# Where the two parts of the norm's operand lie in a partition, and the experts' stationary tiles

## The reference

```python
def rmsnorm(x, g):
    x32 = x.astype(jnp.float32)
    y = x32 * lax.rsqrt(jnp.mean(x32 * x32, axis=-1, keepdims=True) + EPS)
    return (y * g.astype(jnp.float32)).astype(x.dtype)

def swiglu(x, wg, wu, wd):
    return (jax.nn.silu(x @ wg) * (x @ wu)) @ wd

def moe(x, router, wg, wu, wd):
    ...
    for e in range(N_EXPERTS):
        y = y + gates[..., e:e + 1].astype(x.dtype) * swiglu(x, wg[e], wu[e], wd[e])
    return y
```

## The kernel before

| streamed operand | before | after |
|---|---|---|
| `uh`, k = 0 to 6 | 352 | 352 |
| `uh`, k = 7 | 384 | 384 |
| `ul`, k = 0 to 6 | 480 | 352 |
| `ul`, k = 7 | 0 | 0 |
| `hid`, `gop`, `mp`, `ret`, `mixp`, `plep`, `pleU`: both parts | 96 | 352 |
| `whi`, `wlo` as the streamed operand | 288 | 288 |

## Time and profile before

### The profile page before, as it was taken

One profiled execution on the slowest core, in us unless ns is written; L12 is line 12 of the kernel. 1 busy time (PEld: TensorE's weight loads), 2 busy tenths in 40 slices (PEclk: granted clock), 3 DMA queues, 4 the chain that ended last, 5 costly groups with the idle time before them and its releaser, 6 DMA issues.

```text
span 2169.2 us, 37238 instructions
## 1 busy us (share of the span) xinstructions
PE 2112.1 (97%) x15426; PEld 1971.2 (91%) x15426; DVE 1529.8 (71%) x2191; ACT 1366.4 (63%) x1887; POOL 65.4 (3%) x102
## 2 busy tenths in 40 slices
PE   8999999999999999999999999999989999999999
PEld 7988999999989899998888888888879999978999
DVE  5777556765567675565999999976867665875664
ACT  6765475544567654755877777776756545775553
POOL 0003000000000130000000000000000000000000
PEclk9999999999999999998999999999999999999999
DMA  7434345566554343453989999954315565423553
GB/s 262 152 99 138 100 148 177 183 183 193 166 169 149 101 141 97 151 181 149 343 323 329 333 330 333 350 190 156 122 49 180 183 199 164 156 69 127 195 185 136
DMA packets 126450, 400.69 MB, mean 185 GB/s; under 512 B 26048, under 2 KB 26432, under 8 KB 126272
## 3 DMA queue, kind: packets, MB, share of 16 engines
q1 hardware_dynamic: 126272, 398.20, 55.1%
HBM read 395.79 MB, written 2.36 MB: 184 GB/s over the span
## 4 chain that ended last, share of the span: by engine, by line
PE 86%; ACT 6%; DVE 5%; issue 1%; POOL 1%; DMA 0%; SPq 0%; ACTq 0%; DVEq 0%; POOLq 0%
PE ps L492 85%; DVE wlo L2164 2%; ACT scr L1411 2%; ACT whi L1401 1%; ACT arena L1411 1%; DVE arena L2172 1%; DVE arena L2164 1%; DVE scr L2164 1%; ACT L1411 1%; ACT L1405 0%; PE ps L1084 0%; ACT rst L1411 0%; DVE h L2164 0%; ACT uh L1411 0%; POOL arena L3134 0%
## 5 line engine op out<-in xcount | busy, mean ns | idle before, releaser
L2164 DVE TENSOR_TENSOR wlo<-raw,whi 128x1024 fp32r<-128x1024 f32 (+2 forms) x622 | 746.1, 1213 | 288.8 <-ACT whi L1401 283.5
L1401 ACT ACTIVATE whi<-raw 128x1024 fp32r<-128x1024 f32 (+2 forms) x622 | 642.9, 1042 | 315.1 <-PE ps L492 310.0
L492 PE MATMUL ps<-uh,whi 128*128 128x256 f32 x2240 | 647.5, 289 | 12.6 <-DVE arena L2172 4.2
L492 PE MATMUL ps<-uh,wlo 128*128 128x256 f32 x2240 | 633.1, 283 | 0.0
L492 PE MATMUL ps<-ul,whi 128*128 128x256 f32 x2240 | 626.8, 280 | 0.0
L492 PE MATMUL ps<-arena_r,whi 128*128 128x256 f32 x2720 | 477.5, 280 | 2.9 <-DVE arena_r L2164 2.0
L492 PEld LDWEIGHTS ps<-uh,whi 128*128 128x128 f32 x2240 | 421.3, 188 | 25.7 <-issue 14.7
L492 PEld LDWEIGHTS ps<-ul,whi 128*128 128x128 f32 x2240 | 422.9, 189 | 5.6 <-issue 5.3
L492 PEld LDWEIGHTS ps<-arena_r,whi 128*128 128x128 f32 x2720 | 415.0, 189 | 6.8 <-DVE arena_r L2164 3.4
L492 PEld LDWEIGHTS ps<-uh,wlo 128*128 128x128 f32 x2240 | 420.5, 188 | 0.0
L492 PE MATMUL ps<-arena_r,wlo 128*128 128x256 f32 x1360 | 378.3, 278 | 0.0
(11 more groups left out here) (183 smaller groups left out, 2229.4 us busy)
## 6 DMA issues: line engine op xcount, KB each, us to landing
raw<-stream SPq DMA_DIRECT2D x586, 512.0 KB, 4.2
arena<-stream SPq DMA_DIRECT2D x64, 512.0 KB, 5.8
CO<-stream SPq DMA_DIRECT2D x44, 512.0 KB, 5.4
raw<-stream SPq DMA_DIRECT2D x32, 384.0 KB, 4.3
arena<-stream SPq DMA_DIRECT2D x20, 384.0 KB, 4.2
CO<-stream SPq DMA_DIRECT2D x12, 384.0 KB, 4.6
CO<-const SPq DMA_DIRECT2D x2, 704.5 KB, 6.1
h<-xT SPq DMA_DIRECT2D x4, 256.0 KB, 5.8
```

Of the source, the lines that this page charges most:

```text
L492: return self.e.matmul(o, l, r, start=start, stop=stop, skip_group_check=True)
L1401: self.e.activation(M.whi[:, b:b + n], M.raw[a][:, 0:n], ACT.Copy).then_inc(K.sem("weight_hi"), 1)
L2164: return self.e.tensor_tensor(o, a, b, op)
```

## The change

`Tiles` gets its step as an argument: `uh` keeps 8 numbers for tile 7, `ul` gets 8 + 32 = 40 (160 bytes). Both tensors grow from 2080 to 2176 numbers (8704 bytes, 17 x 512), so that `ul` starts at byte 108832 and its tiles 0 to 6 lie like those of `uh` modulo 512. The router's two parts move from tensors of their own into the last 64 numbers of `uh` and `ul`. All that is made later moves up by 256 bytes: the scratch tensors, and the arena from byte 136288 to 136544. In the arena, `UG[0]` becomes two dense tensors of 2048 numbers that begin at 288 modulo 512 (before: 160 and 288, with a last tile 32 bytes further), and `HT` behind them starts 32 numbers further in the arena. No instruction is added, taken away or moved, and no wait.

```diff
--- before.py
+++ after.py
@@ -22,6 +22,8 @@
 AHEAD = 3
 OFF = 16
 STEP = 8
+TURN = 32
+LINE = 128
 ARENA = 23128
 CAP = 128
 ALL = slice(None)
@@ -180,22 +182,19 @@
 
 
 
-    def __init__(self, ap, c0=0, c1=T):
-        self.ap, self.c0, self.c1 = ap, c0, c1
+    def __init__(self, ap, step):
+        self.ap, self.step = ap, step
 
     def __getitem__(self, ix):
 
         p, k, c = ix
-        c0, c1 = self.c0 + (c.start or 0), self.c1 if c.stop is None else self.c0 + c.stop
+        c0, c1 = c.start or 0, T if c.stop is None else c.stop
         if isinstance(k, slice):
             assert k.stop == k.start + 2 and k.start % 2 == 0
-            n = T + (STEP if k.stop == 8 else 0)
+            n = T + (self.step if k.stop == 8 else 0)
             return v3(self.ap[p, k.start * T:k.start * T + 2 * n], n)[:, :, c0:c1]
-        at = k * T + (STEP if k == 7 else 0)
+        at = k * T + (self.step if k == 7 else 0)
         return self.ap[p, at + c0:at + c1]
-
-    def columns(self, c0, c1):
-        return Tiles(self.ap, c0, c1)
 
 
 class Steps:
@@ -297,10 +296,10 @@
         self.SM, self.CO = sb("SM", small_layout()[1]), sb("CO", const_layout()[1])
         raw = sb("raw", NRAW * CH)
         self.whi, self.wlo = sb("whi", NSPLIT * CH, F32R), sb("wlo", NSPLIT * CH, F32R)
-        self.h, uh, ul = sb("h", 2048), sb("uh", 2048 + 2 * OFF, F32R), sb("ul", 2048 + 2 * OFF, F32R)
-        self.hT, self.U = v3(self.h), tuple(Tiles(x[:, OFF:2048 + 2 * OFF]) for x in (uh, ul))
+        self.h, uh, ul = sb("h", 2048), sb("uh", 2048 + LINE, F32R), sb("ul", 2048 + LINE, F32R)
+        self.hT, self.U = v3(self.h), tuple(Tiles(x[:, OFF:2048 + LINE], n) for x, n in ((uh, STEP), (ul, STEP + TURN)))
         self.identr = sb("ident_r", P, F32R)
-        self.router = [v3(sb(x, 64, F32R), 8) for x in ("router_hi", "router_lo")]
+        self.router = [v3(x[:, 2048 + LINE - 64:2048 + LINE], 8) for x in (uh, ul)]
         self.scrs, self.rsts = sb("scr", 7 * 512), sb("rst", 2 * 512)
         self.eps, self.flag = sb("eps", 4), sb("flag", 1, I32)
         with nc.sbuf_tensor("arena", [P, ARENA], F32) as t:
@@ -343,9 +342,9 @@
         self.rows8r = ARr[0:8, 20672 + 4 * T:20672 + 5 * T]
         self.uN = [ARr[:, i * 2048:(i + 1) * 2048].rearrange("p (t d) -> p t d", t=2) for i in range(2)]
 
-        at = 4096 + OFF
-        self.UG = [[Tiles(ARr[:, at + i * (2048 + 2 * OFF):at + (i + 1) * (2048 + 2 * OFF)]) for i in range(2)], self.U]
-        at += 2 * (2048 + 2 * OFF)
+        at = 4096 + LINE - OFF
+        self.UG = [[v3(ARr[:, at + i * 2048:at + (i + 1) * 2048]) for i in range(2)], self.U]
+        at += 4096
         self.HT = [v3(ARr[:, at + i * 1408:at + (i + 1) * 1408], P) for i in range(2)]
         self.YP = [ARr[:, 17600 + i * 1024:18624 + i * 1024] for i in range(2)]
         self.SEL = v3(ARr[:, 19648:20160])
@@ -1061,7 +1060,7 @@
 
     def gate_up(self, w, s, work, e, c):
         f0, n = c * 512, min(512, 1408 - c * 512)
-        ug = [x.columns(e % 2 * P, e % 2 * P + P) for x in self.M.UG[e // 2 % 2]]
+        ug, tokens = self.M.UG[e // 2 % 2], slice(e % 2 * P, e % 2 * P + P)
         for g, name in enumerate(("exp_w_gate", "exp_w_up")):
             b = self.bank(work, "gu", w, e, c, g)
             for k0 in range(0, 8, 2):
@@ -1069,7 +1068,7 @@
                 for k in range(2):
                     for part in range(2):
                         self.wait_ge(*self.K.when("ug", w, e // 2, part, (k0 + k) // 2))
-                    last = self.mm3(b[:, 0:n], pick(ug, ALL, k0 + k, ALL), pick(wt, ALL, k, ALL), k0 + k == 0, k0 + k == 7)
+                    last = self.mm3(b[:, 0:n], pick(ug, ALL, k0 + k, tokens), pick(wt, ALL, k, ALL), k0 + k == 0, k0 + k == 7)
                 done = [("used", i) if w == "main" else ("over used", i)]
                 if k0 == 6:
                     done.append(("ps", "gu", w, e, c, g))
```

## The result

| | before | changed |
|---|---|---|
| median of 20 runs | 2170.42 us | 2176.42 us |
| lowest and highest | 2162.45, 2174.74 | 2168.41, 2181.85 |
| span of the profiled execution | 2169.2 us | 2173.5 us |

The account below looks back on a forecast made before the run. TensorE's distance of matmul starts was taken as the bound. Gains of 9 + 3.7 = 12.7 us off the profiled 2170.99 gave 2158.3, or 2154.0 against the median 2166.85; range 2143 to 2170 us.

Parts of the forecast that it names:

- What bounds the kernel: TensorE, busy 97% of the span, keeps one of two rhythms on alike operands: 113.3 or 118 ns a matmul.
- Case (a): Norm's last tile straight into the hidden product: a place change without pause, costing some 9 and 4 ns, then 113.3 ns.
- rival 1: Norm's operand: rhythm turns only every other time, or mixed stretches give nothing; about 5 us gained, 2162; chance 13%.
- The norm's operand: Alike tiles 0 to 6: groups of 2745 instead of 2833 ns, saving 9 us in dense and 3.7 in mixed stretches.
- The arena: hid, gop and mp, now at 352 and entered by 32 bytes, stay at 113.3 ns: 0; otherwise 10.4 us lost.
- rival 3: Steps into the arena and behind tile 7: 32 bytes don't turn the rhythm; +10.4 us, 2177; chance 14%.
- The experts: Experts' stretch with UG[0] as stationary operand, both parts at 288: 0 gained, bounds -1 to +1 us.
- The cover that I named: Experts' stretch: weights set its time, moving 336 GB/s with DMA engines 93% busy, so TensorE waits for them.
- The rule of the Trainium skill: Counter-argument: TensorE has separate read ports and never waits on anyone, so no place matters and the change gives nothing.
- the losing side: The outcome that the changed kernel is slower by more than 6.5 us; chance 14%.

Follow-up runs that it names:

- r5: Changed kernel with the low part's tile 6 alone moved 128 bytes further besides tile 7, tiles 0 to 5 alike; 2154.49 us, ratio 0.9931 to before.
- y1: Changed kernel with 256 bytes of space ahead of h: norm's operand and arena at 96 modulo 512, steps kept; 2177.57 us, ratio 1.0039 to before.
- y3: Changed kernel with 256 bytes of space ahead of the arena alone: arena back at 96, step of 288 bytes into it; 2179.03 us, ratio 1.0044 to before.
- r2: Changed kernel with TURN = 0: the low part's last tile alike too, at 384 as the high part's; 2177.51 us, run once.
- r1: Changed kernel with the low part's tiles 0 to 6 back at 480 modulo 512, arena still at 352; 2166.10 us, ratio 0.9979 to before.
- r9: Kernel with the low part's tiles 4 to 7 unlike, changed further by OFF = 0: norm's operand at 288, the weights' place; 2171.06 us, run once.
- r4: Changed kernel with the low part's tiles 4 to 6 moved 128 bytes further besides tile 7, tiles 0 to 3 alike; 2156.09 us, ratio 0.9945 to before.
- r3: Changed kernel with STEP = 0 and TURN = 0: all eight tiles of both parts at 352, no step anywhere; 2177.20 us, run once.
- y4: Kernel before with the experts' part of the change alone: UG[0] dense, both parts and HT at 288 modulo 512; 2165.19 us, ratio 0.9980.
- y5: Kernel before with the experts' part alone, but both dense parts and HT at 352 modulo 512 instead of 288; 2173.31 us, run once.

## Why the prediction was wrong

**What bounds the kernel** was right: TensorE's distance of starts, two rhythms on the same bytes, kept from one matmul to the next. **Case (a)** was read wrongly. Its rows hold the last tile only, and I took for the cause what stood in them: "That last step is the one of case (a) with the same three matmuls ahead of it; only its size differs". The failed step is "with the same three matmuls ahead of it". All eleven entries also had unlike tiles 0 to 6 ahead, which the change makes alike. The change and r5 have those three matmuls and that step alike and differ in one unlike tile ahead of them; one stays at 2833 ns a group and the other goes to 2753. So what hands on the tight rhythm reaches further back than tile 7, and the change removed it. The doubt of rival 1, that tile 7 was never seen entered tight, was sound too: with alike tiles ahead, such a stream came out loose in all fifteen cases of the changed kernel, y1, y3 and r2.

**The norm's operand** (9 and 3.7 us): measured 0, 2833 ns a group before and after. The size was nearly right where the turn works, in another layout: I had 2745 ns for a group, r5 has 2753; its first matmul takes 117 or 118 and the next ones 113.3, as written.

**The arena** (0, or +10.4 by rival 3): measured +12.2. Rival 3 names the right place (no triple of 0.34 from the first matmul of `down` on) and a wrong cause: r1 has the step of 32 bytes and is tight, y3 has that of 288 and is loose. That its 2177 lies so near to 2176.42 is luck. It starts from a median of three runs that lies 3.6 us below the one of twenty, it has nothing for the experts' 4.3 us the other way, and its 2,356 matmuls are too few: starts followed one by one, the tight stretches of before hold some 2,750, with the two behind a pause (layer 0's `gop` and `mp`), of which the sum left out one.

**The experts** (0, bounds -1 to +1): measured -4.3. The term looked at `UG[0]` alone and left out `HT`, which moves too and belongs to 528 of the 912 matmuls. The cover that I named, weights from HBM that set the time at 336 GB/s, wasn't one: with the stretch's matmuls 5 ns shorter it moved 339 to 340 GB/s and ended earlier. I had read a busy DMA share as a bound and hadn't asked which wait ends last.

**The rule of the Trainium skill** (SBUF — State Buffer, "Who interferes with whom"), read as the prediction read it, would have had no change at all. The runs disagree with that reading: the place of one tile of 128 x 256 numbers moves the whole by some 21 us. They don't disagree with the sentence itself, which is about engines that wait for each other: within the unbroken streams compared here no trace shows TensorE waiting for one. What stalls, a port, a bank or the order of two requests, none of these runs shows.

**The chances.** I gave the losing side 14%, on the ground that every entry seen was tight. Eleven of eleven was one observation, not eleven: all had the same history.

## What to carry to other kernels

Where a pattern precedes an effect every time, list everything that is the same each time, not only the last instruction, and give each item that the change touches its own rival. In a kernel made of back-to-back matmuls, measure the distance of starts for each pair of operands. Where it has two values for the same bytes, the order of places in the stream ahead is a tuning knob: r5 and the changed kernel lie 1% apart by the position of one tile. Take what starts behind a pause from several traces, since two of the same kernel can differ there. And a stretch with its DMA engines 93% busy may still be paced by another engine; shorten that one by a known amount before calling it covered.

## What the runs showed of the hardware

- Matmuls of 256 columns in float32r against a new 128 x 128 stationary operand each time run at 113.3, 117.7 or 120 ns from start to start at the full clock (1.00), by places modulo 512 bytes and by what ran ahead; with 512 columns it is 227.4 or 232 to 233 ns, and 230.1 in r9.
- A streamed operand whose two parts are alike modulo 512 keeps either rhythm for as long as nothing breaks it, up to 175 triples in a row (the first hidden product). In none of the traces do parts 128 bytes apart hold the tight one.
- One unlike tile ahead of tile 7 (r5), three (r4) or seven (r1 and before), and then a step of 32 bytes (r1, r4, r5) or of 288 (before), turn the alike stream behind them to tight, at a cost of about 9 and 4 ns on two matmuls, at all eleven entries (nine in r5); an alike stream with the same last tile and step doesn't turn (the change, y1, y3). It ends a tight one instead (15 of 15, r2 included), and without a step (r3) a tight one goes on. Why the one and not the other stays open.
- The unbroken group of 24 matmuls takes 2833 ns in the kernel before and in the changed one, in y1 to y3, r1 and r2, though the distances within are spread otherwise (122, 116, 122 around tile 7, or one of 125 behind it). Only without any step is it 2827, or 2720 where it is tight.
- Behind a pause of 1.00 us or an fp32 product the rhythm of a stream can differ between two executions of the same kernel (r4).
- 512 columns streamed from 288 take 227 ns against stationary tiles at 288 (the change, y4) or 32 (y3), and 232 to 233 at 352 (y5) or 416 (`HT` before), though all of these are dense and alike.
- Not tried: unlike tiles in the middle of the operand, which could turn the groups that start behind a pause, and r5 together with other places for the experts' second half, which uses the norm's operand at 352 and stays at 233 ns.
